# Decay matrices of a Gated-DeltaNet layer: built from gamma rows stored and loaded back, in place of replicated copies and triangle products

## What is computed

```python
g = -jnp.exp(gdn_A_log.astype(f32)) * jax.nn.softplus(gd_a.astype(f32) + gdn_dt_bias.astype(f32))
...
gam = jnp.cumsum(g, axis=-1)
diff = gam[..., :, None] - gam[..., None, :]
dec_incl = jnp.exp(jnp.where(incl, diff, -jnp.inf))
```

## Time and profile before

| | |
|---|---|
| three runs | 918.52, 921.14 and 921.93 us, median 921.14 |
| span of the profiled execution | 918.0 us |
| what lies around a span, against the three runs | 0.5 to 3.9 us (3.1 against the median) |
| TensorE busy | 803.6 us, 88% of the span |
| VectorE, ScalarE, GpSimd busy | 482.8, 320.2, 341.2 us |
| DMA | 46.89 MB, 51 GB/s on average |

### The profile page before, as it was taken

The page is one execution under the profiler, slowest core; times in us unless marked ns, Lnnn a source line. Parts: engine busy times, 40 slices in busy tenths (PEclk is TensorE's granted clock), DMA queues, the critical chain, the costliest instruction groups (busy, mean ns, idle before and its releaser), DMA issues. The chain is left out here.

```text
span 918.0 us, 15166 instructions
## 1 busy us (share of the span) xinstructions
PE 803.6 (88%) x5418; PEld 753.3 (82%) x5418; DVE 482.8 (53%) x1052; ACT 320.2 (35%) x835; POOL 341.2 (37%) x458
## 2 busy tenths in 40 slices
PE   2499978999998889999978898999878968999983
PEld 2279978899997789899978898999878967988862
DVE  3454668834333788342336883433368828322237
ACT  3444523333433233325232333352324345411114
POOL 2415356633012566330125662301256526112206
PEclk9999999999999899999998999999989988999987
DMA  2302021022100310110002103300050044125024
GB/s 92 143 4 59 9 69 32 7 41 44 28 1 16 70 38 10 35 44 24 1 22 64 38 10 44 41 17 1 21 73 7 10 140 163 62 94 171 1 96 202
DMA packets 51173, 46.89 MB, mean 51 GB/s; under 512 B 3026, under 2 KB 45844, under 8 KB 51108
## 3 DMA queue, kind: packets, MB, share of 16 engines
q1 hardware_dynamic: 51108, 45.95, 18.7%
HBM read 35.79 MB, written 10.16 MB: 50 GB/s over the span
## 5 line engine op out<-in xcount | busy, mean ns | idle before, releaser
L214 PE MATMUL proj<-uTh,w_high 128*128 128x352 f32 (+1 forms) x768 | 275.4, 359 | 15.9 <-issue 10.6
L214 PE MATMUL proj<-uTh,w_low 128*128 128x352 f32 (+1 forms) x768 | 248.8, 324 | 0.0
L214 PE MATMUL proj<-uTl,w_high 128*128 128x352 f32 (+1 forms) x768 | 248.2, 323 | 0.0
L214 PEld LDWEIGHTS proj<-uTh,w_high 128*128 128x128 f32 x768 | 147.8, 192 | 17.5 <-issue 17.1
L214 PEld LDWEIGHTS proj<-uTl,w_high 128*128 128x128 f32 x768 | 147.7, 192 | 0.0
L214 PEld LDWEIGHTS proj<-uTh,w_low 128*128 128x128 f32 x768 | 146.3, 190 | 0.0
L232 POOL TENSOR_TENSOR w_low<-w_raw,w_high 128x256 fp32r<-128x256 f32 (+1 forms) x66 | 82.2, 1246 | 163.6 <-ACT w_high L224 163.4
L1138 PE MATMUL mix<-level_x 128*128 128x128 f32 x448 | 67.4, 284 | 20.0 <-DVE level_x L994 12.5
L1138 PEld LDWEIGHTS mix<-level_x 128*128 128x128 f32 x448 | 61.0, 195 | 26.6 <-issue 18.9
L1039 DVE SCALAR_TENSOR_TENSOR conv_out<-conv_in,hg_taps,conv_out 128x352 f32<-128x352 f32 (+1 forms) x108 | 75.1, 695 | 1.3
L1549 DVE COPY_PREDICATED gd_n<-mask_ts,mix 128x384 f32<-128x384 uint8 (+1 forms) x60 | 34.4, 572 | 63.5 <-PE mix L1615 61.2
(11 more groups left out here) (288 smaller groups left out, 1466.3 us busy)
## 6 DMA issues: line engine op xcount, KB each, us to landing
w_raw<-in_w_in SPq DMA_DIRECT2D x32, 512.0 KB, 8.6
x_tile<-in_x SPq DMA_DIRECT2D x8, 512.0 KB, 8.5
w_raw<-y_scratch SPq DMA_DIRECT2D x8, 448.0 KB, 4.7
out_y<-w_raw SPq DMA_DIRECT2D x4, 512.0 KB, 2.7
hg_q<-in_w_out SPq DMA_DIRECT2D x2, 512.0 KB, 4.6
hg_th<-in_w_out SPq DMA_DIRECT2D x2, 512.0 KB, 5.3
hg_v<-in_w_out SPq DMA_DIRECT2D x2, 512.0 KB, 6.9
hg_z<-in_w_out SPq DMA_DIRECT2D x2, 512.0 KB, 6.2
```

What stands on the lines that cost most here:

```text
L214: last = pe.matmul(acc[:, 0:tw], w[j % 2][:, k, :], u[:, k, t0:t0 + tw], start=(k == 0 and i == 0), stop=(k == KT - 1 and i == 2))
```

## The change

The 12 GpSimd copies and the 36 triangle products go. In their place gamma (128 partitions x 36) is transposed once on TensorE, copied to the SBUF tile `gamma_rows` (36 x 128), stored to a scratch tensor in DRAM, and loaded back with four DMAs, one for each head, each of which writes that head's 1152 values to all 128 partitions of `decay`. VectorE now subtracts in place in `decay`, and ScalarE takes the exponential in place. The block's parts are shared out anew: 16 instead of 4 stand behind the gamma product, 4 or 3 instead of 5 or 4 behind each dec step.

```diff
-    for key in [("ab", 0), ("gam", 0)] + ...
-        n = {"ab": 20, "gam": 4, "dec": 5 if key[1] < 8 else 4}[key[0]]
+        n = {"ab": 20, "gam": 16, "dec": 4 if key[1] < 8 else 3}[key[0]]
...
 # SP
-            for n in range(2, 5):
-                load_weights(sp, n - 1, tile_cols("hg", n, 0) if n < 4 else tile_cols("gd", 0, 0))
+            load_weights(sp, 1, tile_cols("hg", 2, 0))
+            freed(sp, p2, "rows")
+            sp.dma_start(gam_dram, gamT[:, :]).then_inc(gam_stored, 16)
+            sp.wait_ge(gam_stored, 16)
+            for h in range(HEADS):
+                sp.dma_start(DT[:, h, :], gam_dram[h * NC:(h + 1) * NC, :].rearrange("(a c) t -> a (c t)", a=1).broadcast_to([P, NT])
+                             ).then_inc(dec_in[h], 16)
+            load_weights(sp, 2, tile_cols("hg", 3, 0))
+            load_weights(sp, 3, tile_cols("gd", 0, 0))
...
 # GpSimd
-            pool.wait_ge(gate_step, 9)
-            replicate(0)
-            replicate(1)
             for n in range(HEADS * NG):
                 if n in (1, 5):
                     split_low(pool, 2 + n // 4)
-                if n + 2 < HEADS * NG:
-                    replicate(n + 2)
...
 # ScalarE, dec n
-                freed(act, p2, ("dec", n))
-                act.activation(DT[:, h, g * GW:(g + 1) * GW], dtmp[:, n % 2, :], ACT.Exp).then_inc(dec_exp, 1)
+                act.wait_ge(dec_sub, n + 1)
+                act.activation(DT[:, h, g * GW:(g + 1) * GW], DT[:, h, g * GW:(g + 1) * GW], ACT.Exp).then_inc(dec_exp, 1)
...
 # VectorE
             link(dve.tensor_copy(gam[:, :, :], src))
+            dve.tensor_copy(gamT[:, :], full(dve, p2, "rows")[0:HEADS * NC, 0:P]).then_inc(bank_free(p2, "rows"), 1)
...
-                src = full(dve, p2, ("dec", n))
-                if n >= 2:
-                    dve.wait_ge(dec_exp, n - 1)
-                for i in range(GC):
-                    c = g * GC + i
-                    last = dve.tensor_scalar(dtmp[:, n % 2, i * P:(i + 1) * P], src[:, i * P:(i + 1) * P],
-                                             gam[:, h, c:c + 1], 0.0, ALU.subtract, ALU.min)
-                last.then_inc(bank_free(p2, ("dec", n)), 1)
+                if g == 0:
+                    dve.wait_ge(dec_in[h], 16)
+                for c in range(g * GC, (g + 1) * GC):
+                    d = DT[:, h, c * P:(c + 1) * P]
+                    last = dve.tensor_scalar(d, d, gam[:, h, c:c + 1], 0.0, ALU.subtract, ALU.min)
+                last.then_inc(dec_sub, 1)
...
 # TensorE
+            pe.wait_ge(gate_step, 10)
+            ap, done = take(pe, p2, "rows")
+            pe.transpose(ap[0:HEADS * NC, 0:P], gam[:, :, :].rearrange("p h c -> p (h c)"), ident[:, :]).then_inc(done, 1)
             for n in P2_PARTS[("gam", 0)]:
                 project_part(pe, n)
             for n in range(HEADS * NG):
-                pe.wait_ge(gate_rep, n + 1)
-                ap, done = take(pe, p2, ("dec", n))
-                for i in range(GC):
-                    last = pe.matmul(ap[:, i * P:(i + 1) * P], rep[:, n % 2, i, :], tri[:, :], start=True, stop=True)
-                last.then_inc(done, 1)
                 for m in P2_PARTS[("dec", n)]:
                     project_part(pe, m)
```

More of the change, by code:

```diff
@@ L505, in hybrid_layer @@
     gam = sb("gamma", [P, HEADS, NC], F32, s2)
-    rep = sb("g_rep", [P, 2, GC, P], F32, s2)
-    dtmp = sb("decay_tmp", [P, 2, GW], F32, s2)
+    gamT = sb("gamma_rows", [HEADS * NC, P], F32, s2)
+    gam_dram = nc.dram_tensor("gamma_scratch", [HEADS * NC, P], F32, kind="Internal").ap()
     ones = sb("ones", [P, P], F32, s2)
@@ L512, in hybrid_layer @@
     sw = sb("shift_work", [P, 3, HEADS, NC], F32, s2)
-    p2_names = [("ab", g) for g in range(NG)] + ["gam", "tot"] + [("dec", n) for n in range(HEADS * NG)]
-    p2_names.insert(p2_names.index(("dec", 2)), "down")
-    p2_names.insert(p2_names.index(("dec", 4)), "up")
+    p2_names = [("ab", g) for g in range(NG)] + ["gam", "tot", "rows", "down", "up"]
     p2 = Bank(p2_names)
@@ L525, in hybrid_layer @@
         ones_set, pm0, gate_step, mask_step, mask_set = sem("ones_set"), sem("pm0"), sem("gate_step"), sem("mask_step"), sem("mask_set")
-        gate_exp, gate_rep, dec_exp = (sem(n) for n in
-                                                         ("gate_exp", "gate_rep", "dec_exp"))
+        gate_exp, dec_sub, dec_exp = (sem(n) for n in ("gate_exp", "dec_sub", "dec_exp"))
+        gam_stored, dec_in = sem("gam_stored"), [sem(f"dec_in{h}") for h in range(HEADS)]
         @block.sync
@@ L554, in _ @@
                                base=-PAD, pattern=[[1, 1]], channel_multiplier=1).then_inc(pm0, 1)
-            def replicate(n):
-                h, g = divmod(n, NG)
-                if n >= 2:
-                    full(pool, p2, ("dec", n - 2))
-                pool.tensor_copy(rep[:, n % 2, :, :],
-                                 g_in[:, h, g * GC:(g + 1) * GC].unsqueeze(2).broadcast_to([P, GC, P])).then_inc(gate_rep, 1)
             def level_masks(i):
```

## The result

The changed kernel takes 937.63 us (median of four runs, 932.36 to 939.52) against 921.06 us (918.52 to 921.93): a ratio of 1.0171, 95% interval 1.0138 to 1.0204. It is slower by 1.7%, four times the 0.4% that was forecast, and the time lies above the range.

What follows compares the result with a forecast made beforehand. TensorE's queue was taken to bound the block; removed products gave 7.2 us, but waiting for late load 2 made the block 3.6 us longer. Span 918.0 + 3.6 = 921.6, plus 3.1 around it: 924.7 us, range 918 to 932.

Steps and rivals of the forecast that it cites:

- Blocks after this one are unchanged and simply start later: Blocks behind the second block: no change of their own, only a later start, with 3.6 us added to the span.
- Removing the products gives about 7 us: Second block, TensorE: 8.0 us of triangle products removed, 0.8 us added for the transpose, 7.2 us shorter without other waits.
- Load 2 is late and holds ScalarE, and through the gate columns VectorE and TensorE: Second block: load 2 queues behind store and four loads; its rounding precedes the gate columns, so three engines wait.
- T = 94.0: Landing time of load 2 in the second block, put at 94.0 us, bounds 87.3 and 102.7; break-even 90.4.
- my two bounds: Rate of the four gamma loads: 234 GB/s taken, ending at 91.2 us; other bound 418 GB/s, ending at 86.7.
- T + 3.95 until TensorE goes on: Second block: TensorE goes on 3.95 us after load 2 lands, at 97.95, having been idle 8.8 us.
- Clock, 1.7 us: Second block: lower granted clock after TensorE's wait costs its first work 1.7 us; bounds nothing and twice as much.
- The block 3.6 us longer: Second block ends on ScalarE at 119.6 us instead of 116.0, 3.6 us later.
- Rival 1: Load 2 moved at its own pace after the four loads, landing 99.7 to 102.7; time 930.4 to 933.4; chance 0.18.
- rival 2: Four loads at 418 GB/s, or load 2 mixing with them: landing 88.5 to 91.5, time 919.2 to 922.2; chance 0.23.
- 3: Rival without stall: load 2 lands below 87.5, gain comes through; time 913.9, 914.3 or 916.3 us; chance 0.06.

Runs made afterwards that it cites:

- e2: The kernel before the change with 103 semaphore increments at the start of TensorE's program, none of the change: 936.05 us, ratio 1.0181 to before.
- e1: The changed kernel with 153 semaphore increments at the start of TensorE's program: 928.39 us, ratio 1.0066 to before.
- e8: The changed kernel with 40 semaphore increments at the start of TensorE's program: 923.77 us, ratio 1.0022 to before.
- e3: The changed kernel with load 2 issued ahead of the store of gamma: 930.51 us, ratio 1.0096 to before.
- e7: The kernel before the change with 60 semaphore increments at the start of TensorE's program: 924.05 us, ratio 1.0028 to before.
- e6: The changed kernel with 8 parts instead of 16 behind the gamma product, 5 or 4 behind dec steps, and 90 increments at TensorE's start: 918.07 us, ratio 0.9961.
- e9: The changed kernel with load 2 ahead of the store and 40 semaphore increments at TensorE's start: 914.31 us, ratio 0.9934 to before.
- e4: The changed kernel with load 2 ahead of the store and 153 semaphore increments at TensorE's start: 921.41 us, ratio 1.0008 to before.

## Why the prediction was wrong

The step that failed is "Blocks after this one are unchanged and simply start later". They are unchanged in code and data, but not in where their code lies. The 153 instructions that the change takes out of TensorE's program move the loop over the heads so that a new piece of instructions begins 17 instructions behind the first weight load of a pass. There TensorE waits a second time after the jump, 6.3 and 8.7 us, and works at the lower clock meanwhile; with it the two blocks took 16.2 us longer. e2 shows it without any of the change, e1 and e8 show the changed kernel without it. No rival of mine had it. The size of the second wait could not be read from the trace of before; the 5.1 and 5.5 us issue waits in front of the second and third pass were there to see, and I took them for a fixed cost.

Of the other steps, each with its measurement:

- *Removing the products gives about 7 us.* Right: with load 2 in time (e3) the block ended 6.3 us earlier than before. Ahead of the gamma products the granted clock was 0.84 in e3 and 1.00 in the trace of before; against e2 and e7, the old kernel at 0.84 (end at 116.7), it is 7.0 us.
- *Load 2 is late and holds ScalarE, and through the gate columns VectorE and TensorE.* Right, shown by e3 and e6.
- *T = 94.0.* It was 92.4. The store was issued at 78.90, 1.1 us later than I put it, and took 1.35 us up to the first load at 80.25, where I put 2.2; the last of the four loads landed 8.1 us after 81.6, at 89.7, where I put 91.2. Their rate was 270 GB/s at first and 415 after, between my two bounds, so the 234 GB/s that I took for all of it, from a single load, was too low. Load 2 followed 2.7 us later; I had 2.8.
- *T + 3.95 until TensorE goes on.* 96.18, T + 3.8. TensorE had reached the place at 89.9, not 89.2, and idled 6.25 us, not 8.8.
- *Clock, 1.7 us.* Too small: at 0.50 from 96 to 102, about 2.7 us of work were lost, where the nearest wait of before had cost 1.7.
- *The block 3.6 us longer.* 2.9 us, and 2.2 us by its end against e2 and e7 at the same clock ahead of gamma. The whole kernel with the code at a harmless place, e8, is at 923.8, where I forecast 924.7.
- *Rivals.* Rival 1 (load 2 hardly prepared) did not happen, nor did rival 2 or 3.

**What stays open.** After a jump the second packet of instructions started 6.8 to 11.8 us after the first, and what sets this was not tried; SP issues the block's weight loads at the same time. The 50 instructions between my count and the waits are read from the waits alone: some of them stand between the loop's start and the first weight load, and for the others I have no reason. The second block began its gamma products at 77.5 instead of 76.2 in the changed kernel, with a granted clock from 66 to 77 of 0.84 where the trace of before has 1.00. This is not the change's doing: the old kernel has 0.84 and 77.1 in e2 and e7, and e9, with the change, has 1.00. Why the clock differs there is open.

## What to carry to other kernels

- When a change moves a load behind a store and its completion, ask which engine takes that load next and what is queued behind it there. Here no engine waited for the four new loads' own data. The load behind them held the gate columns only because a new share of filler work (parts) had put its rounding ahead of them.
- Time that changes in code that did not change has to be looked up by block, before the change is judged. With waits of kind "issue" behind a loop's jump, pad the program by a few dozen instructions, on the old kernel too: 14 to 15 us moved with the place of the code alone (e2 against before, e8 against the changed kernel). Then count the instructions between the two waits: few of them ahead of a new piece are what hurts. A pad costs 0.16 us an increment where it isn't hidden.

## What the runs showed of the hardware

- Four loads in a row, each of 4608 bytes of DRAM to all 128 partitions, moved 263 and 277 GB/s in their first four us and 415 GB/s in the next two, at full busy share in both.
- TensorE waited 5.1 to 5.8 us before the first matmul of the second and of the third pass of a loop of 2563 instructions (by the built program) in every kernel. The wait ended 2.4 to 2.9 us after a 16 KB packet of instructions had started.
- A second wait followed 17 instructions behind the first weight load (4.9 to 8.7 us) or 60 behind it (1.1 and 1.8 us), depending on the place of the loop in its program, and none where the next piece was an estimated 120 instructions away or more.
- 103 semaphore increments in a row took until 16.76 us on TensorE and did not delay the second block (e2); 153 took until 24.39 us and delayed it by 6.5 (e1) and 5.3 us (e4).
